# A conditioned hybrid decoder step on one core: the first norm's mean inside the second modulation group, small loads on another queue, high sample parts by VectorE

## What is computed

```python
def rmsnorm(x, g):
    xf = x.astype(jnp.float32)
    y = xf * lax.rsqrt(jnp.mean(xf * xf, axis=-1, keepdims=True) + NORM_EPS)
    return (y * g.astype(jnp.float32)).astype(x.dtype)
...
    for l in range(DEPTH):
        ada = jax.nn.silu(c) @ w_ada[l] + b_ada[l]
        sh1, sc1, gt1, sh2, sc2, gt2 = jnp.split(ada[:, None, :], 6, axis=-1)
        h = rmsnorm(x, norm1_g[l]) * (1.0 + sc1) + sh1
        mix, sr, sl, sc = mixer(h, pos, s_ret[l], s_lru[l], s_conv[l], w_in[l], w_proj_ret[l],
                                w_proj_lru[l], w_out[l], conv_w[l], conv_b[l], w_rg_a[l], b_rg_a[l],
                                w_rg_x[l], b_rg_x[l], lru_lambda[l])
        x = x + gt1 * mix
        h2 = rmsnorm(x, norm2_g[l]) * (1.0 + sc2) + sh2
        x = x + gt2 * (jnp.square(jax.nn.relu(h2 @ w_mlp1[l])) @ w_mlp2[l])
```

## Time and profile before

| | us |
|---|---|
| median of 3 runs | 2083.71 |
| lowest and highest run | 2083.22, 2085.11 |
| profiled execution | 2082.57 |
| its span, first to last instruction | 2080.8 |
| TensorE busy in the span | 2055.0 |
| VectorE, ScalarE, GpSimd busy | 1063.9, 726.0, 231.9 |

### The profile page before, as it was taken

One profiled execution on the slowest core, in us unless ns is written; L12 is line 12 of the kernel. 1 busy time (PEld: TensorE's weight loads), 2 busy tenths in 40 slices (PEclk: granted clock), 3 DMA queues, 4 the chain that ended last, 5 costly groups with the idle time before them and its releaser, 6 DMA issues.

```text
span 2080.8 us, 35363 instructions
## 1 busy us (share of the span) xinstructions
PE 2055.0 (99%) x14880; PEld 1939.3 (93%) x14880; DVE 1063.9 (51%) x1675; ACT 726.0 (35%) x916; POOL 231.9 (11%) x241
## 2 busy tenths in 40 slices
PE   6999999999999999999999999999999999999998
PEld 3869989999998999999988798999999899999998
DVE  5615566674446444444464355667635453535353
ACT  4125444665323222122231354456632321212122
POOL 0001120000031001000320011100000320101014
PEclk8999999999999999999999999999999999999999
DMA  8523242222262232323521314322222622222223
GB/s 351 183 71 106 91 158 95 79 82 82 81 243 102 82 122 82 122 82 122 207 98 62 111 65 139 132 79 87 79 81 81 238 73 90 82 82 82 82 82 107
DMA packets 78920, 232.62 MB, mean 112 GB/s; under 512 B 7360, under 2 KB 27840, under 8 KB 78528
## 3 DMA queue, kind: packets, MB, share of 16 engines
q1 hardware_dynamic: 56448, 205.15, 27.9%
q10 hardware_dynamic: 22336, 25.49, 3.7%
HBM read 218.52 MB, written 12.09 MB: 111 GB/s over the span
## 4 chain that ended last, share of the span: by engine, by line
PE 97%; DVE 2%; DMA 1%; ACT 0%; SPq 0%; issue 0%; DVEq 0%; POOL 0%
PE acc L1292 81%; PE acc L1444 4%; PE misc L1375 2%; PE misc L1563 1%; PE acc L1345 1%; DMA first_raw<-ada_in 1%; PE misc L1524 1%; PE misc L1453 1%; PE acc L1353 1%; PE misc L1497 1%; PE misc L1500 1%; DVE tmp L841 1%; PE misc L1386 0%; PE misc L1499 0%; DVE h_lo L827 0%; PE misc L1517 0%
## 5 line engine op out<-in xcount | busy, mean ns | idle before, releaser
L417 ACT ACTIVATE weight_h<-raw 128x1024 fp32r<-128x1024 f32 x286 | 303.1, 1060 | 1082.5 <-PE acc L1292 980.3
L1292 PE MATMUL acc<-h_hi,weight_h 128*128 128x288 f32 x2688 | 583.0, 298 | 0.0
L1292 PE MATMUL acc<-h_hi,weight_l 128*128 128x288 f32 x2688 | 575.5, 296 | 0.0
L1292 PE MATMUL acc<-h_lo,weight_h 128*128 128x288 f32 x2688 | 575.2, 296 | 0.0
L799 DVE TENSOR_TENSOR weight_l<-raw,weight_h 128x1024 fp32r<-128x1024 f32 x286 | 398.1, 1392 | 261.3 <-ACT weight_h L417 260.8
L1292 PEld LDWEIGHTS acc<-h_hi,weight_h 128*128 128x128 f32 x2688 | 433.4, 189 | 10.2 <-issue 6.5
L1292 PEld LDWEIGHTS acc<-h_lo,weight_h 128*128 128x128 f32 x2688 | 432.8, 189 | 0.0
L1292 PEld LDWEIGHTS acc<-h_hi,weight_l 128*128 128x128 f32 x2688 | 432.8, 189 | 0.0
L1292 PE MATMUL acc<-b_hi,weight_l 128*128 128x288 f32 x1520 | 325.5, 296 | 0.0
L1292 PE MATMUL acc<-b_hi,weight_h 128*128 128x288 f32 x1520 | 325.5, 296 | 0.0
L1292 PE MATMUL acc<-b_lo,weight_h 128*128 128x288 f32 x1264 | 270.6, 296 | 0.0
(11 more groups left out here) (226 smaller groups left out, 1885.9 us busy)
## 6 DMA issues: line engine op xcount, KB each, us to landing
raw<-stream SPq DMA_DIRECT2D x290, 512.0 KB, 3.5
ada_raw<-ada_in SPq DMA_DIRECT2D x48, 512.0 KB, 6.3
first_raw<-ada_in SPq DMA_DIRECT2D x36, 512.0 KB, 14.3
s_s<-state_in ACTq DMA_DIRECT2D x8, 1024.0 KB, 6.9
ret_s_out<-s_s ACTq DMA_DIRECT2D x8, 1024.0 KB, 4.6
two_raw<-ada_in SPq DMA_DIRECT2D x12, 512.0 KB, 10.6
x<-x_in ACTq DMA_DIRECT2D x1, 2304.0 KB, 13.4
wrg<-wrg_in ACTq DMA_DIRECT2D x18, 128.0 KB, 2.9
```

The costliest lines, as they stand in the source:

```text
L417: A(weight_h[:, j % 2, :], raw[:, (j + 2) % 4, :], ACT.Copy).then_inc(h_split, 1)
L1292: last = M(acc[j % 2][:, half, 0:HALF], w, r[:, k, half * HALF:(half + 1) * HALF], start=(k == 0 and n == 0), stop=(k == KT - 1 and n == 2))
```

## The change

Five edits, all in the prologue of layer 0.

- The five small loads (`fg`, `lru_c`, `conv_c`, twice `wrg`) are requested by SyncE behind the tables instead of by ScalarE.
- TensorE computes the mean of squares inside group 1, between its second and third load (`between` of `ada_group`), and spreads the root directly behind the first turn, ahead of group 2.
- ScalarE loads the table of the root and takes the root ahead of the copy of group 1's row, and copies the row of group 3 between the sixth and seventh scaling tile instead of behind the eighth.
- VectorE splits weight tile 1 and takes the reciprocal ahead of the scale and of the samples' scaling.
- The high part of the samples is written by a new VectorE instruction, the addition of the shift with `h_hi` as its output (semaphore `first_samples`); ScalarE's copy in `high` goes for the first norm. The counts on `h_rounded` change by one for it (`rounded`), in the later norms without effect on the order.

```diff
@@ -295,6 +296,10 @@
+        def rounded(n):
+
+            return n * 9 + 1
@@ -344,6 +349,10 @@
             sp.dma_start(const[:, NFIRST:NCONST], const_in[:, NFIRST:NCONST]).then_inc(tables_loaded, 16)
+            for dst, src in [(fg[:], fg_in), (lru_c[:], h0_in), (conv_c[:], conv_in)]:
+                sp.dma_start(dst, src).then_inc(params_loaded, 16)
+            for t in range(2):
+                sp.dma_start(wrg[:, t, :], wrg_in[t]).then_inc(wrg_loaded[t], 16)
@@ -453,8 +458,8 @@
                 for m in range(KT):
                     act.wait_ge(xn_ready, n * 9 + (m + 2 if n and m else m + 1))
                     A(prompt(one(h_hi, m)), prompt(one(tmp, m)), ACT.Identity, bias=column(ada, m + shift_at)).then_inc(h_rounded, 1)
-                    if m == 0:
-                        act.wait_ge(xn_ready, n * 9 + (2 if n else 9))
+                    if m == 0 and n:
+                        act.wait_ge(xn_ready, n * 9 + 2)
                         A(samples(h_hi), tmp_s(n), ACT.Copy).then_inc(h_rounded, 1)
@@ -476,15 +481,16 @@
+                    act.wait_ge(c_cleared, 1)
+                    load_root_table()
+                    norm_std(0)
                     ada_row_out(0)
-                    load_root_table()
                     ada_sum_out(0)
                     act.wait_ge(scales_ready, 1)
                     for m in range(KT):
-                        if m == 4:
-                            norm_std(0)
+                        if m == 6:
+                            ada_row_out(1)
                         scale_tile(m, scale1)
-                    ada_row_out(1)
                     ada_sum_out(1)
@@ -815,24 +821,29 @@
             def shift_samples(n, shift_at):
 
+                if n == 0:
+                    V.tensor_tensor(by_sample(h_hi), by_sample(tmp), to_samples(ada[:, shift_at:shift_at + KT, :]), ALU.add).then_inc(first_samples, 1)
                 dst = tmp_s(n).rearrange("p k a (b t) -> p k a b t", t=DS)
@@ -858,6 +869,8 @@
                 if lay == 0:
                     first_split(0)
+                    first_split(1)
+                    root(0)
@@ -1339,7 +1352,9 @@
                         if j == 0:
-                            pe.wait_ge(h_rounded, n * 9 + k + 2)
+                            pe.wait_ge(h_rounded, rounded(n) + k)
+                        if n == 0 and k == 0:
+                            pe.wait_ge(first_samples, 1)
@@ -1404,11 +1419,10 @@
                     ada_group(0, 0, first_raw[0], first_loaded[0])
-                    ada_group(1, 0, first_raw[1], first_loaded[1])
+                    ada_group(1, 0, first_raw[1], first_loaded[1], first_mean)
                     turn(0)
-                    first_mean()
+                    spread_root(0)
                     ada_group(2, 0, first_raw[2], first_loaded[2])
-                    spread_root(0)
                     ada_group(3, 0, first_raw[3], first_loaded[3])
```

More of the change, by code:

```diff
@@ L244, in build @@
         u_ready, u_rounded, u_split = sem("u_ready"), sem("u_rounded"), sem("u_split")
+        first_samples = sem("first_samples")
         half_done, x_last, last_chain = sem("half_done"), sem("x_last"), sem("last_chain")
@@ L408, in _ @@
             A(e_neg, tmp[:, 3, 0:16], ACT.Exp, scale=-1.0).then_inc(setup_act, 1)
[L409 to L412, removed]
             def split_h(lay, off, i, j):
@@ L821, in low @@
             def low(n, shift_at):
-                dve.wait_ge(h_rounded, n * 9 + 2)
+                if n == 0:
+                    dve.wait_ge(first_samples, 1)
+                    dve.wait_ge(xn_ready, 9)
+                else:
+                    dve.wait_ge(h_rounded, rounded(n))
                 V.tensor_tensor(samples(h_lo), tmp_s(n), samples(h_hi).bitcast(F32), ALU.subtract).then_inc(h_ready, 1)
                 for m in range(KT):
-                    dve.wait_ge(h_rounded, n * 9 + (m + 2 if m else 1))
+                    dve.wait_ge(h_rounded, rounded(n) + m)
                     V.scalar_tensor_tensor(prompt(one(h_lo, m)), prompt(one(tmp, m)), column(ada, m + shift_at), prompt(one(h_hi, m)).bitcast(F32),
@@ L832, in norm @@
                 scale_samples(n, x, scale)
-                if n == 0:
-                    first_split(1)
-                root(n)
+                if n:
+                    root(n)
                 dve.wait_ge(s_scaled, 2 * n + 1)
```

## The result

| | before | changed |
|---|---|---|
| median of 22 runs each, us | 2083.11 | 2080.05 |
| lowest and highest | 2082.50, 2085.11 | 2078.93, 2082.83 |
| profiled execution | 2082.57 | 2080.42 |
| its span | 2080.8 | 2078.5 |

The forecast was 2.9 us.

The account below looks back on a forecast made before the run. TensorE bounds nearly everything except the prologue, where two chains end together. Shortening both moves the first projection matmul from 40.21 to 37.35, 2.86 us, so 2083.71 becomes 2080.8 (profiled 2079.7); range 2079.3 to 2083.2.

Parts of the forecast that it names:

- two chains: Prologue: the mean-to-samples chain and the group 3 load chain end within about half a microsecond; a gain needs both shortened.
- Part 1, the loads: Prologue loads: moving five small loads behind the tables lands group 3's last load 1.89 us earlier, at 32.72.
- Part 2, the mean: TensorE, inside group 1: mean of squares starts at 21.37 instead of 25.84 and ends at 25.99.
- Parts 3 and 4: After the mean: scaling starts at 29.86; ScalarE copies group 3's row before tiles 6 and 7; chains meet at 36.5.
- Part 5, the samples: End of prologue: one VectorE addition writes the samples' high part until 37.2; TensorE starts 0.13 us later, at 37.35.
- Sum: First projection matmul moves from 40.21 to 37.35, 2.86 us; nothing behind it moves relative to TensorE.
- The clock stays up: Projection start: TensorE's clock does not fall in the shorter pause; gain 3.6 us, 2080.1; chance 0.22.
- the clock rises late: Group 1: TensorE stays at 1.2 GHz until about 25.9, mean ends near 27.8; gain 1.4, 2082.3; chance 0.10.
- The loads do not land earlier: Group 3 done at 35.75, tiles 6 and 7 behind its copy, projection at 39.2; gain 1.0, 2082.7; chance 0.10.
- The small loads come too late: VectorE's first rotary product waits for them; at twice the shared time it costs 8.8 us, 2089.6; chance 0.03.

Follow-up runs that it names:

- loads alone: Kernel before, with only the five small loads moved to SyncE's queue behind the tables; 2083.49 us beside 2083.20 for before.
- order alone: Changed kernel with the small loads back on ScalarE's queue and the samples' high part by ScalarE, as before; 2082.39 us beside 2083.01 for before.
- samples alone: Kernel before, with only the high part of the samples written by VectorE; 2082.06 us beside 2083.01 for before.
- repetition: The changed kernel unaltered, run once more beside other kernels on the same chip; 2080.14 us beside 2083.20 for before.
- loads back: Changed kernel with the five small loads moved back to ScalarE's queue; 2081.88 us beside 2083.20 for before.
- samples back: Changed kernel with the high part of the samples copied by ScalarE again; 2080.83 us beside 2083.80 for before.
- early filler: Changed kernel with two unused-result matmuls ahead of group 1 alone; 2080.09 us beside 2083.80 for before.
- both fillers: Changed kernel with two unused-result matmuls ahead of group 1 and two behind the turn of group 3; 2079.10 us beside 2083.20 for before.
- pause filler: Changed kernel with two unused-result matmuls behind the turn of group 3 alone; 2079.29 us beside 2083.80 for before.

## Why the prediction was right, point by point

**The two chains.** The prediction's main claim, that the prologue has two chains which end within half a microsecond and that a gain needs both shortened, is what the runs with single parts show most clearly. By the first projection matmul (40.21 in the kernel before), the loads alone give 0.17 us, the order alone 0.28, the samples alone 0.77, together 1.2; the whole change gives 2.4, and 2.1 in its repetition. The rest exists only when loads and order come together: order and samples without the loads (loads back) give 1.00, which is the sum of the two. One trace seems to say otherwise, that of samples back, which has loads and order and gives 0.19; its mean ended at 28.42, 1.6 us later than in the changed kernel and 2.0 later than with the order alone, and its time by median is 3.0 us below before. So the sizes of such sums are good to about a microsecond, while the waits in the traces (1.81 us of ScalarE at the copy with the order alone, none with the loads) show the mechanism itself.

**Part 1, the loads.** Forecast: last load of group 3 at 32.72; measured 32.96, so 1.65 us earlier instead of 1.89. The rate taken from spacings of landings was nearer than the one by bytes (1.3; the loads are 548 KB, not the 544 of the prediction, which changes nothing). That the small ones are cheap on their own queue was read rightly too: in 1.5 us behind the tables, against 8.6. The Trainium skill, page "DMA: Bandwidth & Descriptors", section "Queues, rings and completion order", has each DMA engine alternate between queues packet by packet; the two durations agree with that, though no run here separates it from other costs of short packets.

**Part 2, the mean.** Forecast end 25.99, measured 26.82. The step that was off is the clock: it was assumed to rise at 22.5 as in the trace before and rose at 24.0, so that the mean took 5.28 us and not 4.6. That is 0.66 of the 0.83 us; the other 0.17 is the start, 21.54 instead of 21.37. In the traces of the experiments with the same order it took from 4.74 to 6.21 us, and 4.10 where the early filler stood ahead of it.

**Parts 3 and 4.** From the end of the mean to the start of the scaling 3.87 us were forecast and 3.89 measured; from there to the meeting of the chains 6.6 and 6.2. Of the difference only 0.09 is the copy's wait for TensorE's group 3, which the forecast had (33.77 to 33.86) and the trace has not. The rest are lengths on ScalarE: the copy began 3.69 us behind the first scaling tile, where the forecast counted 3.91 for the six tiles alone, and the next tile began 0.48 us behind the copy, where it counted 0.65. The copy came late itself (34.40, the group was done at 34.04), because the late mean had pushed the scaling. So the loads had 0.36 us of slack in this execution, and 0.04 in the repetition. With the early filler, which gives a mean of 4.10 us, ScalarE does wait for TensorE at this copy, for 1.72 us with both fillers.

**Part 5, the samples.** From the shift to TensorE 0.85 us were forecast (36.5 to 37.35) and 0.90 measured; the saving of the part, by the prediction's own numbers 1.49 less 0.85, 0.64, is 0.60 to 0.65.

**Sum.** Forecast 37.35 and 2.86 us; measured 37.82 and 2.39 in this pair of traces, 3.06 by medians. That the place was missed by only 0.47 is in part luck: the late mean cost 0.83, and the shorter way behind the scaling gave 0.4 of it back. That the medians came within 0.2 us of the forecast is in part luck too, since the medians mix executions with different clocks and the forecast was made for one. The profiled execution of before was one of the short ones of its kernel (2082.57 in a range from 2082.50), that of the changed kernel one of the long half of its (2080.42, median 2080.05), so that the two differ by 2.15 only. In the repetition the medians differ by 3.06 again, while the traced execution, with its 9.37 us of slow projection, is 0.5 us faster than that of before.

**The rivals.** "The clock stays up" was called a rival with a chance of 0.22, and "the clock rises late" one with 0.10. The runs point to both as states of the same program, with the median between them, but neither was caught whole in a trace of the changed kernel. The clock stayed up in the kernel with the loads back (7.03 us), and there it was worth 0.85 us against the 7.88 of before, where 0.7 were forecast. For the changed kernel it is inferred: its runs near 2079.1 leave 44.6 for the end of the 48 matmuls, as with both fillers (37.66 and 7.01), and with 8.06 us they would have to start at 36.5, earlier than in any trace. The clock rose as late as 26.5 in samples back; in the changed kernel it rose at 24.0. For the 48 matmuls the 13 traces show 7.0 to 7.1 us four times, 7.9 to 8.2 six times, 8.9 once and 9.3 to 9.4 twice; the prediction did not have the last two. The Trainium skill, page "TensorE: Matmul & The Clock Gate", section "Part 1: The HAM clock gate", says that the monitor runs freely and a kernel's slow part differs from run to run; the pair of executions of one program at 8.06 and 9.37 us agrees. "The loads do not land earlier" fell, and the place it gave, 39.2, is where the kernel with the loads back stood (39.21). "The small loads come too late" fell with about 7 us to spare.

## What to carry to other kernels

Where two chains meet, a part that shortens one is worth little alone and much beside a part that shortens the other: take single parts out of the changed kernel before judging them, and don't only put them into the old one. Small loads that are not needed soon belong behind the large ones on the same queue: beside them, on another queue, they delayed the last large one by 1.65 us here, where the estimate by their bytes gives 1.3. After a short pause of TensorE compare several executions, not one trace, take the length of the matmuls behind the pause into the sum, and consider filling the pause with matmuls whose result nobody reads, ending them before the awaited work arrives.

## What the runs showed of the hardware

TensorE's clock fell in a pause of 1.66 us in two executions of one program and did not in a pause of 1.67 us of another kernel (loads back). Once down, it was back at 2.4 GHz after 3.2 us of dense matmuls in one execution and after about 6 us in the other, with the same matmuls. That second duration was not expected, and it cost 1.3 us more. With fillers at both places the projection and the mean ran at 2.4 GHz in the one trace taken (7.01 and 4.10 us). The granted clock can read 1.00 while the matmuls have the lengths of 1.2 GHz, as in the mean of the pause filler's trace (6.01 us).
